# Finer pieces and another order of work in the front stage of a two-block transformer kernel

## The reference, cut to what matters

```python
mod = jax.nn.silu(c) @ ada_w[layer] + ada_b[layer]
shift1, scale1, gate1, shift2, scale2, gate2 = [m[:, None, :] for m in jnp.split(mod, 6, axis=-1)]
u = rms_norm(h, norm1_g[layer]) * (1 + scale1) + shift1
z = u @ w_in[layer]
q_a, kc, vc, ksl, vsl, kwn, vwn, g_a, q_b, k_b, v_b, m_a, m_b = jnp.split(z, split_at, axis=-1)
q_a = rms_norm(q_a.reshape(B, S, NSA_HEADS, HEAD_DIM), q_norm_g[layer])...
k_cmp = rms_norm(compress_blocks(kc.reshape(kv_shape), ...), k_norm_g[layer, 0])
```

## Time and profile before

| what | value |
| --- | --- |
| runs | 1910.49, 1910.87, 1914.55 us; median 1910.87 |
| profiled execution | 1914.49 us, its span 1912.6 us |
| PE busy | 1686.8 us (88%) |
| DVE, ACT, POOL busy | 753.9, 480.5, 213.4 us |
| mean granted TensorE clock | 0.95 of full speed |

### The profile page before, as it was taken

The page is one execution under the profiler, slowest core; times in us unless marked ns, Lnnn a source line. Parts: engine busy times, 40 slices in busy tenths (PEclk is TensorE's granted clock), DMA queues, the critical chain, the costliest instruction groups (busy, mean ns, idle before and its releaser), DMA issues. The chain is left out here.

```text
span 1912.6 us, 20343 instructions
## 1 busy us (share of the span) xinstructions
PE 1686.8 (88%) x7854; PEld 1121.1 (59%) x7855; DVE 753.9 (39%) x1289; ACT 480.5 (25%) x797; POOL 213.4 (11%) x269
## 2 busy tenths in 40 slices
PE   3879999989899899999997999889599999987872
PEld 2768887766444677878886778767333333332321
DVE  6334322655465677613325455353411111111113
ACT  4212333546000422222224442251211111110001
POOL 4010000000011222210003000002211111110001
PEclk9989998979899999999998999899699999999996
DMA  9422220020544577422230222105889977999994
GB/s 292 128 67 66 88 88 23 1 89 1 198 157 153 196 264 245 173 88 88 88 107 15 87 88 66 67 1 209 335 357 425 427 316 303 426 426 426 426 412 159
DMA packets 99423, 362.03 MB, mean 189 GB/s; under 512 B 19967, under 2 KB 23211, under 8 KB 87027
## 3 DMA queue, kind: packets, MB, share of 16 engines
q1 hardware_dynamic: 90543, 344.95, 47.4%
q0 software_dynamic: 5760, 9.02, 1.3%
q10 hardware_dynamic: 3012, 6.59, 1.0%
HBM read 357.75 MB, written 14.75 MB: 195 GB/s over the span
## 5 line engine op out<-in xcount | busy, mean ns | idle before, releaser
L2170 PE MATMUL x_upa<-x_ring,x_Ta 128*64 128x512 f32 x608 | 137.4, 605 | 22.2 <-DMA x_ring<-in_w_expert_up_dram 22.2
L2170 PE MATMUL x_gpa<-x_ring,x_Ta 128*64 128x512 f32 x608 | 139.7, 613 | 18.6 <-DMA x_ring<-in_w_expert_gate_dram 16.9
L2170 PEld LDWEIGHTS x_upa<-x_ring,x_Ta 128*64 128x64 f32 x608 | 46.9, 139 | 110.6 <-issue 110.6
L2170 PEld LDWEIGHTS x_gpa<-x_ring,x_Ta 128*64 128x64 f32 x608 | 47.6, 141 | 108.3 <-issue 108.3
L322 DVE TENSOR_TENSOR p_lo<-p_raw,p_hi 128x2048 fp32r<-128x2048 f32 x18 | 41.3, 2292 | 145.1 <-ACT p_hi L626 145.1
L329 PE MATMUL fr_p<-p_hi,u_high 128*128 128x512 f32 x224 | 89.1, 398 | 0.0
L330 PE MATMUL fr_p<-p_lo,u_high 128*128 128x512 f32 x224 | 88.0, 393 | 0.0
L331 PE MATMUL fr_p<-p_hi,u_low 128*128 128x512 f32 x224 | 88.0, 393 | 0.0
L2226 ACT ACTIVATE x_siga<-x_gpa 128x512 f32<-128x512 f32 x19 | 11.3, 597 | 260.8 <-PE x_gpa L2170 260.8
L2191 PE MATMUL x_y0a<-x_ring,x_aTa 128*64 128x512 f32 x304 | 69.4, 598 | 6.6 <-ACT x_aTa L2231 3.3
L626 ACT ACTIVATE p_hi<-p_raw 128x2048 fp32r<-128x2048 f32 (+1 forms) x20 | 37.4, 1871 | 135.0 <-DMA p_raw<-in_w_in_dram 135.0
(11 more groups left out here) (770 smaller groups left out, 3827.7 us busy)
## 6 DMA issues: line engine op xcount, KB each, us to landing
x_ring<-in_w_expert_gate_dram SPq DMA_DIRECT2D x32, 2048.0 KB, 27.3
x_ring<-in_w_expert_up_dram SPq DMA_DIRECT2D x32, 2048.0 KB, 27.4
x_ring<-in_w_expert_down_dram SPq DMA_DIRECT2D x32, 2048.0 KB, 29.8
p_raw<-in_w_in_dram SPq DMA_DIRECT2D x18, 1024.0 KB, 5.1
adaw0m<-in_w_ada_dram SPq DMA_DIRECT2D x6, 2048.0 KB, 10.6
adaw1m<-in_w_ada_dram SPq DMA_DIRECT2D x6, 2048.0 KB, 9.8
fr_ada<-in_ada_w_dram SPq DMA_DIRECT2D x4, 2048.0 KB, 15.4
w_raw0m<-in_mlp_w_dram SPq DMA_DIRECT2D x8, 1024.0 KB, 7.0
```

The source lines that it names most:

```text
L2170: mm = nc.tensor.matmul(ps[CAP * f:CAP * f + CAP, :], self.xT[:, k, CAP * f:CAP * f + CAP], w[m + f][:, k, :], start=(k == 0), stop=(k == ...
```

## The change

- The first unit of the modulation is loaded in two pieces and each other unit in four (`PIECES`), each piece with a semaphore of its own; `add_up` becomes `add_part`, which waits piece by piece. The weights of half step 0 are loaded ahead of unit 1.
- All low parts are made on DVE. The four of u's first half are interleaved with the four pieces of unit 2. ACT casts the weights of half step 0 ahead of the scaling of x. TensorE turns four row groups in one go.
- Half steps 0 and 1 run by row group, with the banks inside (`first_half`), and wait for each row group's low part alone.
- `q_stats` runs tile by tile, each tile with a power of its own on POOL, with the work on the compressed keys between. `q_turn(0)` and (1) are in gap(6), (2) and (3) in gap(7); `q_take(2)` and (3) are at the head of beside(9).

```diff
+PIECES = [[(0, 4), (4, 8)]] + [[(2 * j, 2 * j + 2) for j in range(4)]] * 3
...
                 def unit(u):
                     m, n = units[u]
-                    sp.dma_start(wbuf[u][:, :, :], eights(ada_w, m * D + 512 * n, 512)).then_inc(ada_in[u], 16)
+                    src = eights(ada_w, m * D + 512 * n, 512)
+                    for j, (k0, k1) in enumerate(PIECES[u]):
+                        sp.dma_start(wbuf[u][:, k0:k1, :], src[:, k0:k1, :]).then_inc(ada_in[u][j], 16)
...
+                weights(0)
                 unit(1)
-                weights(0)
                 unit(2)
...
-                w_low_of(0)
-                for k in range(4):
-                    pool.wait_ge(high_ready, k + 1)
-                    pool.tensor_tensor(lowT[:, k, :], uT[:, k, :], high[:, k, :].bitcast(F32), ALU.subtract).then_inc(low_pool, 1)
-                w_low_of(1)
...
                 pool.wait_ge(q_var, 1)
-                pool.tensor_tensor(rs[:, 0:32], ss[:, 0:32], C.neghalf[:, 0:32], ALU.pow).then_inc(q_rs, 1)
+                pool.tensor_tensor(rs[:, 0:8], ss[:, 0:8], C.neghalf[:, 0:8], ALU.pow).then_inc(q_rs, 1)
                 pool.wait_ge(kc_var, 1)
                 pool.tensor_tensor(crs[:, :], css[:, :], C.neghalf[0:64, 0:1], ALU.pow).then_inc(kc_rs, 1)
+                for t in range(1, NT):
+                    pool.wait_ge(q_var, t + 1)
+                    pool.tensor_tensor(rs[:, 8 * t:8 * t + 8], ss[:, 8 * t:8 * t + 8], C.neghalf[:, 0:8], ALU.pow).then_inc(q_rs, 1)
...
+                act.wait_ge(v_out, 32)
+                w_high_of(0)
+                act.wait_ge(rstd_ready, 1)
+                for j in range(NT):
+                    nc.scalar.activation(xn[:, j, :], C.h[:, j, :], ACT.Copy, scale=rstd[:, j:j + 1]).then_inc(xn_ready, 1)
...
-                act.wait_ge(v_out, 32)
-                w_high_of(0)
                 for k in range(4):
                     take(k)
                     split(k)
...
+                def u_low(k):
+                    dve.wait_ge(high_ready, k + 1)
+                    low(v, lowT[:, k, :], uT[:, k, :], high[:, k, :]).then_inc(low_dve, 1)
...
                     if h == 6:
                         hidden(0)
                         hidden(1)
-                        q_stats()
+                        q_stats(0)
+                        compressed_keys()
+                        q_stats(1)
                         q_norm(0)
+                        q_stats(2)
+                        compressed_keys_scaled()
+                        q_stats(3)
                     if h == 7:
                         q_norm(1)
-                        compressed_keys()
                         q_take(0)
                         q_norm(2)
...
                 add_up(0)
                 dve.wait_ge(squares, NT)
                 v.tensor_scalar(ssq[:, :], ssq[:, :], 1.0 / D, EPS, ALU.mult, ALU.add).then_inc(var_ready, 1)
-                add_up(1)
                 dve.wait_ge(cols_turned, 2)
...
+                dve.sem_inc(cols_kept, 1)
                 to_columns(0)
+                add_up(1)
+                w_low_of(0)
                 to_columns(1)
-                add_up(2)
+                for j in range(4):
+                    add_part(2, j)
+                    u_low(j)
                 add_up(3)
+                w_low_of(1)
                 to_columns(2)
                 to_columns(3)
...
+                def first_half(i):
+
+                    pe.wait_ge(w_low, i + 1)
+                    for k in range(4):
+                        kk = 4 * i + k
+                        pe.wait_ge(low_dve, kk + 1)
+                        for b in range(w[0][1]):
+                            mm = matmul3(nc, bank[b][:, :], (hi[i][:, k, P * b:P * b + P], lo[i][:, k, P * b:P * b + P]),
+                                         (high[:, kk, :], lowT[:, kk, :]), kk == 0, kk == KD - 1)
+                            if kk == KD - 1:
+                                mm.then_inc(bank_ready, 1)
+                    if i == 0:
+                        mm.then_inc(half_used, 1)
...
+                    if h == 6:
                         pe.wait_ge(ga_out, 1)
                         q_turn(0)
-                    if h == 6:
                         pe.wait_ge(kc_ready, 1)
                         nc.tensor.transpose(E0[:, 0:64], kc[:, :], C.ident[0:64, 0:64]).then_inc(kc_turned, 1)
                         pe.wait_ge(vcd_done, 1)
                         q_turn(1)
+                    if h == 7:
                         pe.wait_ge(q_taken, 1)
                         q_turn(2)
-                    if h == 7:
                         pe.wait_ge(q_taken, 2)
                         q_turn(3)
```

More of the change, by code:

```diff
@@ L461, in front @@
         rows_in, cols_turned, v_ready, v_copied, v_out = [sem(n) for n in ("rows_in", "cols_turned", "v_ready", "v_copied", "v_out")]
-        x_in, ada_in = s.sems("fr_x_in", NT), s.sems("fr_ada_in", 4)
-        own, summed, spread, columns = [sem(n) for n in ("own", "summed", "spread", "columns")]
+        x_in, ada_in = s.sems("fr_x_in", NT), [s.sems(f"fr_ada_in{u}", len(PIECES[u])) for u in range(4)]
+        own, summed, spread, columns, cols_kept = [sem(n) for n in ("own", "summed", "spread", "columns", "cols_kept")]
         squares, var_ready, rstd_ready, xn_ready, turned = [sem(n) for n in ("squares", "var", "rstd", "xn", "turned")]
-        out_act, out_dve, high_ready, low_pool, low_dve = [sem(n) for n in ("out_act", "out_dve", "u_high", "u_low_pool", "u_low_dve")]
+        out_act, out_dve, high_ready, low_dve = [sem(n) for n in ("out_act", "out_dve", "u_high", "u_low_dve")]
         w_landed = s.sems("fr_w_landed", 2)
-        w_high, w_low_pool, w_low, half_used, bank_ready, bank_out = [sem(n) for n in (
-            "w_high", "w_low_pool", "w_low", "half_used", "bank_ready", "bank_out")]
+        w_high, w_low, half_used, bank_ready, bank_out = [sem(n) for n in (
+            "w_high", "w_low", "half_used", "bank_ready", "bank_out")]
         cw_in, cw2_in, pos_in, cleared, late_cleared = [sem(n) for n in ("cw_in", "cw2_in", "pos_in", "cleared", "late_cleared")]
@@ L626, in w_high_of @@
                     nc.scalar.activation(hi[i % 2][:, :, 0:n], raw[i % 2][:, :, 0:n], ACT.Copy).then_inc(w_high, 1)
+                for j in range(NT):
+                    act.wait_ge(x_in[j], 16)
+                    nc.scalar.activation(xn[:, j, :], C.h[:, j, :], ACT.Square, accum_out=ssq[:, j:j + 1]).then_inc(squares, 1)
+                act.wait_ge(v_out, 32)
+                w_high_of(0)
+                act.wait_ge(rstd_ready, 1)
+                for j in range(NT):
+                    nc.scalar.activation(xn[:, j, :], C.h[:, j, :], ACT.Copy, scale=rstd[:, j:j + 1]).then_inc(xn_ready, 1)
                 def take(k):
@@ L720, in _, with add_part, add_up @@
                 ch = Chain(dve, own)
-                def add_up(u):
+                def add_part(u, j):
                     a, wb, sc = acc[u % 2], wbuf[u], M[0].sc
-                    dve.wait_ge(ada_in[u], 16)
-                    if u >= 2:
+                    dve.wait_ge(ada_in[u][j], 16)
+                    if j == 0 and u >= 2:
                         dve.wait_ge(spread, u - 1)
[L727 to L730, removed]
+                    for k in range(*PIECES[u][j]):
+                        if k == 0:
+                            ins = v.tensor_scalar(a[:, :], wb[:, 0, :], sc[:, 0:1], None, ALU.mult)
+                        else:
+                            ins = v.scalar_tensor_tensor(out=a[:, :], in0=wb[:, k, :], scalar=sc[:, k:k + 1], in1=a[:, :],
+                                                         op0=ALU.mult, op1=ALU.add)
                         if k < KD - 1:
                             ch.link(ins)
-                    ins.then_inc(summed, 1)
+                    if j == len(PIECES[u]) - 1:
+                        ins.then_inc(summed, 1)
+                def add_up(u):
+                    for j in range(len(PIECES[u])):
+                        add_part(u, j)
+                def u_low(k):
+                    dve.wait_ge(high_ready, k + 1)
+                    low(v, lowT[:, k, :], uT[:, k, :], high[:, k, :]).then_inc(low_dve, 1)
                 def to_columns(u):
@@ L777, in hidden, with q_stats @@
                     ins.then_inc(hid_ready, 1)
[L779 to L784, removed]
+                def q_stats(t):
+                    if t == 0:
+                        dve.wait_ge(bank_out, FRONT_UPTO[2])
+                    part = ss[:, 8 * t:8 * t + 8]
+                    ch.link(v.tensor_tensor(sq[:, :], B.qa[:, t, :], B.qa[:, t, :], ALU.mult))
+                    ch.link(v.tensor_reduce(part, sq[:, :].rearrange("p (h d) -> p h d", d=HD), AX.X, ALU.add))
+                    v.tensor_scalar(part, part, 1.0 / HD, EPS, ALU.mult, ALU.add).then_inc(q_var, 1)
                 def q_norm(t):
-                    dve.wait_ge(q_rs, 1)
+                    dve.wait_ge(q_rs, t + 1)
```

(13 more changed lines are left out.)

22 lines of the change are left out of this document (5 added, 17 removed).

## The result

The changed kernel takes 1899.3 us in the median of five runs (1894.1 to 1906.4), against 1914.55 us of the kernel before (five runs, 1910.5 to 1915.9). The ratio is 0.9926, 95% interval 0.9905 to 0.9947: a gain of under 1%, but clear of the noise. Timed once more beside other kernels (e10) it came to 0.9935 (0.9910 to 0.9961), 13.6 us. The profiled execution took 1895.2 us. The forecast was 1895.1, its range 1889 to 1903; of the difference it forecast 15.75 us, and 15.3 were measured.

The account below looks back on a forecast made before the run. The front stage was taken as bound by TensorE, gaining only from its waits and low clock, with half step 2's weights gating the opening. 2.65 + 13.1 = 15.75 us off the profiled 1910.87 median gave 1895.1 us, range 1889 to 1903.

Parts of the forecast that it names:

- TensorE is 12.7 us ahead, and w(2) is not: Opening: half step 1 starts 12.7 us early, but half step 2's weights gain only 0.2 us, so 5.05 us are won.
- Rival A: Front: TensorE's whole advance, 12.7 + 13.1 = 26 us, comes through, giving 1885 us; 4%.
- wrong if half step 2 starts before 66: Opening: sign set to show the forecast wrong and rival A right; half step 2 was forecast at 68.1.
- Its size: Ahead of half step 2: start at 68.1 instead of 73.15, 5.05 us won, with 7.6 us of new idle time.
- rival C: Opening: loads in pieces are slower, w(2) lands 4.2 us late, the opening's net is -1.5, giving 1899 us; 6%.
- The clock: Half step 2: begins at 1.2 GHz after the idle time, for 4.4 to 6.1 us, costing 2.4 us.
- The opening's net: Opening up to half step 2: 5.05 us won less 2.4 for the clock, 2.65 us; bounds 0 and 5.2.
- The query part: Between half steps 5 and 6: the 11.1 us wait for `fr_qn` and 2.0 us of low clock go, 13.1 us.
- The thin margin of q_norm(1): Half step 6: q_norm(1) is ready at 137.9, its turn asked for at 139.6, 1.7 us to spare.
- rival D: Half steps 6 to 8: VectorE comes too late, a 2 to 6 us wait plus clock, giving 1898 to 1904 us; 13%.
- The small steps: Opening: second unit's sum ends at 26.9 and ScalarE's first `take` starts at about 29.4, 5.2 us earlier.
- This passes to the end: Behind the front: all work there waits for the front, so the 15.75 us gain reaches the kernel's end.

Follow-up runs that it names:

- e10: The changed kernel itself, timed again beside two variants and the kernel before: 1898.85 us, ratio 0.9935 to the kernel before.
- e3: The changed kernel with half steps 0 and 1 bank by bank again, behind all four low parts: 1884.98 us in a single execution.
- e4: The changed kernel with each modulation unit loaded in one 2 MB transfer instead of pieces: 1893.5 us.
- e9: The changed kernel with low parts of u's first half and of half steps 0 and 1's weights made on GpSimd again: 1895.1 us.
- e7: The changed kernel with half step 2's weights loaded once half step 0 is done, ahead of second hidden weights and bias gathers: 1894.9 us.
- e12: The kernel with half step 2's weights loaded earlier in the queue, timed in six executions: 1887.3 us, ratio 0.9872 to the kernel before.
- e1: The kernel before with the query part of the change alone (norms tile by tile, turns a half step later): 1901.9 us.
- e2: The changed kernel with the query norms and turns as they were before: 1915.0 us.
- e6: The changed kernel with 24 matmuls whose result nobody reads put into the idle time ahead of half step 2: 1904.0 us.
- e5: The changed kernel with all query squares first, one power over 32 columns and compressed keys behind, turns still a half step later: 1903.4 us.
- e8: The changed kernel with half step 2's weights loaded earlier and the bias gathers moved behind half step 3's weights: 1889.1 us.

## Why the prediction was right

*The gate.* The step "TensorE is 12.7 us ahead, and w(2) is not" held: 13.0 us at half step 1, 6.7 at half step 2. e3, e4 and e9 give up 5 to 8 us of the opening each and end the front within 2.2 us of the change's 292.26; e7 takes the gate away and 9 us more come (5.6 between e12 and e10). Rival A is out. One sign was set too sharply: "wrong if half step 2 starts before 66". The change's second profile has it at 65.58, with w(2) landing at 61.29 and TensorE still waiting 5.3 us for it.

*Its size.* I put half step 2 at 68.1 and it was at 66.46, because w(2) landed 1.9 us earlier than before and I had allowed 0.2. The idle time ahead was 5.9 us for the weights and 0.5 for the positions, not 7.6. I had argued that the loads could not go faster because the DMA engines were full all the way. Their mean busy share from 40 to 60 us is indeed above one (1.08 before, 1.16 after), but they moved 229 GB/s in that stretch (241 in the second profile) against 207 before, 205 in e1 and 208 in e4, all three with whole units: full did not mean as fast as can be. The profiles with pieces have w(2) mostly 1 to 3 us earlier than those with whole units, the ranges overlapping at 64.05 to 64.42. So the slower loads of rival C did not come. Nor did what the prediction takes for this case from the Trainium skill, "DMA: Bandwidth & Descriptors", section Bandwidth; what little there is points the other way, and the measurement decides.

*The clock.* 4.9 us at the low level in half step 2 (66.46 to 71.3), 2.2 us lost; I had 2.4. It is no fixed price: 2.9 us at the low level in the second profile, 5.3 in e2, behind much the same wait (5.3 and 5.9 us). The opening's net by e2 is 3.0, forecast 2.65; by the change itself, at the end of half step 5, it is 4.3, and 6.0 in the second profile. So this term came out too small in every reading.

*The query part.* Forecast 13.1; e1 has 13.4, or 12.6 without its luck ahead of half step 2, and 12.8 of the change's 17.1 fell behind half step 5. The chain on VectorE came as counted: q_norm(0) was ready at 127.2 and its turn was asked at 134.05, 6.8 us in time (on the time line of before, the forecast had 131.4 and 138.6, which is 7.2 us). The thin margin of q_norm(1), 1.7 us by the forecast, was 1.9 (ready at 133.3, asked for at 135.2). None of rival D's waits came.

*The small steps.* `take` was expected at 29.4 and came at 28.0: the first piece of unit 0 landed at 7.44, w(0) was there at 18.1, so the whole chain ran ahead. With the gate behind it this did not matter.

*The sum.* 15.75 us were forecast. The ruler moved by 17.1 and 19.1, the medians by 15.3 and 13.6. The mechanism was right, but that the total fell within half a us of the first median is partly luck: the opening was put too low, and what the stretch behind the front did to the time was not in the sum.

*Behind the front.* "This passes to the end" is right in the mean, as far as medians can tell, and not in one execution. From the ruler to the issue of the second half of the first block's `w_out` (two attention stages) it took 259.6 us before, 256.1 after, and between 250.9 (e3) and 264.9 (e6) over the fourteen profiles, though nothing there was changed. From there to the first output transfer it was 1333.0 to 1339.5. The two profiles of the changed kernel differ by 8.5 us in the first stretch. The granted clock tells why. Here is that stretch in e3 and in e6, with the clock third from the end:

```profile
291.87:542.78 250.91, 219.51 (x1140) 151.46 (x1140) 145.03 (x352) 99.60 (x241) 17.31 (x20) 0.95 0.23 80
292.16:557.01 264.85, 233.85 (x1140) 163.09 (x1140) 145.01 (x352) 99.73 (x241) 17.32 (x20) 0.89 0.21 76
```

The instructions are the same, and over all fourteen profiles the length follows the clock: 0.95 at 250.9 us, 0.94 at 253.1 and 254.1, 0.93 at 256.1, 0.92 at 258.6, 0.91 at 259.5 to 260.4, 0.90 at 261.8, 0.89 at 264.6 to 264.9. The single times show it too: e2 took 1915.0 us, more than the kernel before, with its front ending 3.0 us earlier; e4 took 1893.5, e5 1903.4, e6 1904.0, e7 1894.9 and e8 1889.1. So a single time can't tell kernels apart that are 10 us different, and the ruler could.

## What to carry to other kernels

When several waits stand in a row on the critical engine, look for the next transfer behind them before adding up what their removal brings: what is gained beyond its landing is idle time, and idle time can cost clock on top. Two of the edits of this opening, undone one at a time, cost nothing that the ruler can tell, and the pieces 2 to 4 us; moving one load ahead of the second hidden weights and the bias gathers in its queue was worth 6 to 9 us there. What is left of such a gate is thin: after the move the next load was 1.9 us late in one of two profiles. A wait for a long side chain is best removed by asking for its result one step later, and then by ordering the chain so that everything asked for in that step is ready, not just the first.

## What the runs showed of the hardware

- TensorE's granted clock fell to 0.50 although TensorE was busy, behind some 8 us of 64x32 matmuls, in e6 and e8, where the stretch had a stall of 0.58 and 0.26 us, and in none of the twelve other profiles, with the same instructions there and stalls of up to 0.25 us. The Trainium skill, "TensorE: Matmul & The Clock Gate", section HAM oscillation, tells of clock losses through waits for data; here the rows show one where hardly any wait was.
- Waits ahead of half steps 2 and 3 were followed by a low clock in some cases and not in others: 3.3 us at 0.50 behind a wait of 1.9 us (e12), 3.4 us behind one of 3.3 (e4, beginning 1.4 us after it had ended), none behind 2.1 us (e9) or 0.9 (e3). Behind 5.3 to 5.9 us it was 2.9 to 5.3 us.
- Splitting 2 MB loads into 512 KB pieces did not cost bandwidth: from 5 to 25 us the engines moved 384 GB/s after and 374 before, and from 28 to 30 us 391 against 384. In the two us from 14 to 16 it was 345 against 397. The first piece, of 1 MB, could be used 5 us earlier than the whole unit.
- Two unchanged attention stages took 250.9 to 264.9 us with the granted clock between 0.95 and 0.89, in step with each other. These 14 us are nearly as much as the whole effect of the change (15.3 us). Where in these stages the clock is lost was not studied.
